# A ten-block transformer kernel: products with ones and with the rotary permutation as two rounded passes

## What is computed

```python
for i in range(2):                       # first block
    x = layer_norm(ALPHA*x + 0.5*swiglu(x, ...))
    x = layer_norm(ALPHA*x + token_mix(x, ...))
    x = layer_norm(ALPHA*x + 0.5*swiglu(x, ...))
    x = layer_norm(ALPHA*x + sigmoid(x @ w_gate + b) * (p[i] @ w_proj))
for l in range(2):                       # second block
    h = x @ w_in[l]                      # MLA and differential attention
    ...
    x = layer_norm(ALPHA*x + merged @ w_out[l])
```

```python
def l2_normalize(t):
    return t * rsqrt(sum(t*t, axis=-1, keepdims=True) + 1e-6)
```

```python
rot = concat([x1*cos - x2*sin, x2*cos + x1*sin])
```

## Time and profile before

| | us |
|---|---|
| median of 3 launches | 1514.75 (1513.74 to 1515.01) |
| the profiled execution, its own time | 1514.83 |
| its span, first to last instruction | 1513.0 |
| TensorE busy | 1496.9 |
| VectorE busy | 947.8 |
| ScalarE busy | 811.1 |
| GpSimd busy | 250.5 |

### The profile page before, as it was taken

One profiled execution on the slowest core, in us unless ns is written; L12 is line 12 of the kernel. 1 busy time (PEld: TensorE's weight loads), 2 busy tenths in 40 slices (PEclk: granted clock), 3 DMA queues, 4 the chain that ended last, 5 costly groups with the idle time before them and its releaser, 6 DMA issues.

```text
span 1513.0 us, 27372 instructions
## 1 busy us (share of the span) xinstructions
PE 1496.9 (99%) x11622; PEld 1384.2 (91%) x11622; DVE 947.8 (63%) x1379; ACT 811.1 (54%) x1249; POOL 250.5 (17%) x140
## 2 busy tenths in 40 slices
PE   9999999999999999999999999999999999999998
PEld 8998898889998889998898989998789999899997
DVE  6655466776555475654558685655477766767756
ACT  6554376545544364554574554544365675555762
POOL 0000252113000260000432040000430004500041
PEclk9999999999999999999999999999999999999999
DMA  9655464236555456555543155555455344553341
GB/s 384 226 195 194 159 210 143 79 110 229 190 196 195 167 204 222 195 195 190 195 173 113 59 190 200 194 195 195 167 209 195 112 140 152 208 188 136 131 149 56
DMA packets 39720, 266.26 MB, mean 176 GB/s; under 512 B 4460, under 2 KB 4716, under 8 KB 9392
## 3 DMA queue, kind: packets, MB, share of 16 engines
q1 hardware_dynamic: 38304, 260.13, 48.8%
q0 software_dynamic: 720, 3.35, 0.6%
q10 hardware_dynamic: 576, 1.05, 0.2%
HBM read 263.46 MB, written 1.05 MB: 175 GB/s over the span
## 4 chain that ended last, share of the span: by engine, by line
PE 94%; DVE 4%; ACT 1%; DMA 0%; issue 0%; SPq 0%; DVEq 0%
PE PS L487 17%; PE PS L488 17%; PE PS L489 16%; PE PS L501 6%; PE PS L503 6%; PE PS L502 6%; PE PS L559 4%; PE PS L562 4%; PE PS L560 4%; PE PS L470 1%; PE PS L471 1%; PE PS L472 1%; PE PS L614 1%; PE PS L1942 1%; DVE rawL L319 1%; PE PS L1351 1%
## 5 line engine op out<-in xcount | busy, mean ns | idle before, releaser
L487 PE MATMUL PS<-xTH,WH 128*128 128x256 f32 x2256 | 641.2, 284 | 0.0
L488 PE MATMUL PS<-xTL,WH 128*128 128x256 f32 x2256 | 628.7, 279 | 0.0
L489 PE MATMUL PS<-xTH,rawL 128*128 128x256 f32 x2256 | 626.6, 278 | 0.0
L316 ACT ACTIVATE WH<-raw 128x1024 fp32r<-128x1024 f32 (+2 forms) x476 | 484.6, 1048 | 131.1 <-PE PS L562 101.3
L319 DVE TENSOR_TENSOR rawL<-raw,WH 128x1024 fp32r<-128x1024 f32 (+1 forms) x395 | 481.4, 1245 | 102.5 <-ACT WH L316 102.2
L487 PEld LDWEIGHTS PS<-xTH,WH 128*128 128x128 f32 x2256 | 423.6, 188 | 9.2 <-issue 6.7
L488 PEld LDWEIGHTS PS<-xTL,WH 128*128 128x128 f32 x2256 | 423.7, 188 | 3.4 <-issue 2.9
L489 PEld LDWEIGHTS PS<-xTH,rawL 128*128 128x128 f32 x2256 | 424.9, 188 | 0.0
L319 POOL TENSOR_TENSOR rawL<-raw,WH 128x1024 fp32r<-128x1024 f32 (+1 forms) x81 | 196.1, 2443 | 1049.8 <-ACT WH L316 1049.8
L316 ACT ACTIVATE sg<-PS 128x256 f32<-128x256 f32 x79 | 30.3, 384 | 177.6 <-PE PS L489 177.6
L319 DVE TENSOR_TENSOR hh<-PS,sg 128x256 f32<-128x256 f32 x79 | 33.5, 424 | 144.7 <-ACT sg L316 144.7
(11 more groups left out here) (366 smaller groups left out, 2004.7 us busy)
## 6 DMA issues: line engine op xcount, KB each, us to landing
raw<-in_weights SPq DMA_DIRECT2D x233, 1024.0 KB, 4.8
gb<-in_lngb SPq DMA_DIRECT2D x16, 512.0 KB, 5.1
raw<-in_weights SPq DMA_DIRECT2D x2, 1056.0 KB, 4.9
gb<-in_ln SPq DMA_DIRECT2D x4, 512.0 KB, 4.5
cst<-in_consts POOLq DMA_DIRECT2D x1, 1378.5 KB, 10.4
x0T<-in_xT ACTq DMA_DIRECT2D x4, 256.0 KB, 5.5
raw<-in_weights SPq DMA_DIRECT2D x4, 256.0 KB, 5.1
xt<-in_x POOLq DMA_DIRECT2D x1, 1024.0 KB, 17.3
```

The source lines that it names most:

```text
L316: return Q.put("act", waits, lambda e: e.activation(out, in_, func, **kw))
L487: e.matmul(out, c, xTH[:, k, :], start=k == 0, stop=False)
L488: e.matmul(out, c, xTL[:, k, :], start=False, stop=False)
L489: ins = e.matmul(out, u.L(i, 128 * k, 128), xTH[:, k, :], start=False, stop=k == KD - 1)
```

## The change

Both kinds of product are now made in two rounded passes. For the squares, ScalarE writes a rounded square `sqH` beside the plain one, VectorE subtracts it from the plain one in place (`sqL`), and TensorE multiplies both with the rounded ones and accumulates. For the rotation, the ScalarE copy `rw` is now the rounded part, VectorE makes the remainder `rl` from PSUM, the cosine product reads PSUM, the bank is released by the copy, the remainder and the cosine product together, and the sine product goes into a tile of its own (`rsum`). The permutation is rounded once a layer. The rounded ones are made once, at the first use, which is the first `squares`. The products with the ones at L1807 to L1809 stay as they are.

```diff
+    ones_ready = []
+
+    def ones_rounded():
+        if not ones_ready:
+            ones_ready.append(act(onesR[:, :], ones, ACT.Copy, [par_ready]))
+        return ones_ready[0]
...
-        o_ = act(onesR[:, :], ones, ACT.Copy, [par_ready])
-        ple_bias[l] = (bgR, o_, stt(bgR[:, :], bgH[:, :].bitcast(F32), C("minus1")[0:2, :], bg[:, :], ALU.mult, ALU.add, [a]))
+        ple_bias[l] = (bgR, ones_rounded(), stt(bgR[:, :], bgH[:, :].bitcast(F32), C("minus1")[0:2, :], bg[:, :], ALU.mult, ALU.add, [a]))
...
+        sqH = [put_at("sqHa", [128, 512], 63, F32R), put_at("sqHb", [128, 512], 65, F32R)]
+        sqL = [put_at("sqLa", [128, 512], 12, F32R), put_at("sqLb", [128, 512], 14, F32R)]
...
                                 if (nm, i) == ("q", 1):
-                                    a = act(sq3, dst, ACT.Square, [a, sq_free[m]])
+                                    y = act(sq3, dst, ACT.Square, [a, sq_free[m]])
                                 else:
-                                    a = tt(sq3, dst, dst, ALU.mult, [a, sq_free[m]], "pool")
-                                conv_ready[nm, i] = (m, a)
+                                    y = tt(sq3, dst, dst, ALU.mult, [a, sq_free[m]], "pool")
+                                h = act(sqH[m][:, :].rearrange("p (j s) -> p j s", j=2), dst, ACT.Square, [a, sq_free[m]])
+                                conv_ready[nm, i] = (m, y, h)
...
         def squares(nm, i):
-            m, a = conv_ready[nm, i]
+            m, y, h = conv_ready[nm, i]
             b, free = bank("B")
-            p = pe([a, free], lambda e: e.matmul(PS[:, b, :], ones, sq[m][:, :], start=True, stop=True))
+            lo = tt(sqL[m][:, :], sq[m][:, :], sqH[m][:, :].bitcast(F32), ALU.subtract, [y, h])
+
+            def fn(e):
+                e.matmul(PS[:, b, :], onesR[:, :], sqH[m][:, :], start=True, stop=False)
+                return e.matmul(PS[:, b, :], onesR[:, :], sqL[m][:, :], start=False, stop=True)
+            p = pe([ones_rounded(), h, lo, free], fn)
...
-        rw = [put_at("rwa", [128, 2, S], 36), put_at("rwb", [128, 2, S], 38)]
+        rw = [put_at("rwa", [128, 2, S], 36, F32R), put_at("rwb", [128, 2, S], 38, F32R)]
+        rl = [put_at("rla", [128, 2, S], 70, F32R), put_at("rlb", [128, 2, S], 72, F32R)]
+        rs_, permR = put_at("rsum", [128, 2, S], 74), put_at("permR", [128, 128], 76, F32R)
...
+        perm_ready = act(permR[:, :], C("perm"), ACT.Copy, [xw])
...
         def rotary(b, p, dst):
...
-            w = rw[i]
+            w, wl = rw[i], rl[i]
             a = act(w[:, :, :], v2(b), ACT.Copy, [p, rw_free[i]])
-            release(b, a)
-            c = tt(pr[:, :, :], w[:, :, :], two(C("dcos")), ALU.mult, [a, pr_free[0]])
+            lo = tt(wl[:, :, :], v2(b), w[:, :, :].bitcast(F32), ALU.subtract, [a])
+            c = tt(pr[:, :, :], v2(b), two(C("dcos")), ALU.mult, [p, pr_free[0]])
+            release(b, a, lo, c)
 
             def later():
                 b2, free = bank("B")
-                p2 = pe([a, free], lambda e: e.matmul(PS[:, b2, :], C("perm"), w[:, :, :].rearrange("p j s -> p (j s)"), start=True, stop=True))
-                s = tt(w[:, :, :], v2(b2), two(C("dsin")), ALU.mult, [p2, c])
+
+                def fn(e):
+                    e.matmul(PS[:, b2, :], permR[:, :], w[:, :, :].rearrange("p j s -> p (j s)"), start=True, stop=False)
+                    return e.matmul(PS[:, b2, :], permR[:, :], wl[:, :, :].rearrange("p j s -> p (j s)"), start=False, stop=True)
+                p2 = pe([perm_ready, a, lo, free], fn)
+                s = tt(rs_[:, :, :], v2(b2), two(C("dsin")), ALU.mult, [p2, c])
                 release(b2, s)
-                y = tt(dst, pr[:, :, :], w[:, :, :], ALU.add, [s, c])
+                y = tt(dst, pr[:, :, :], rs_[:, :, :], ALU.add, [s, c])
```

## The result

The changed kernel takes 1545.31 us (median of 4 launches, 1544.61 to 1546.13), the kernel before 1514.88 in the same comparison: a ratio of 1.0203, 95% interval 1.0185 to 1.0220. It is 30 us slower. The forecast was 1539.6 us with a range of 1532 to 1548.

The account below looks back on a forecast made before the run. TensorE, busy 1496.9 of 1513.0 us, was taken as the bound. Mixer waits less savings gave +24.6 us, the second block +0.2; on the profiled 1514.83 us that made 1539.6 us, range 1532 to 1548.

Parts of the forecast that it names:

- The savings per product: Squares and rotary products: two passes take 0.46 us in place of 0.86, saving 0.40 each, 6.4 us for all 16.
- The rival with 0.42 us a pass: All changed products: passes no cheaper, at 0.42 us each, giving 1545.7 us; chance 0.05.
- The four waits: TensorE before the four squares products of each mixer layer: 2.4, 4.3, 4.3 and 3.15 us, waiting for VectorE's remainder.
- The sum of 24.8 us: Whole kernel: 24.6 us added by two mixer layers plus 0.2 us by the second block.
- The remainder's price of 0.69: VectorE's subtraction in the mixer: 0.69 us, as a multiplication of the same size with both inputs in SBUF.
- the dearer one of 1.21: Mixer remainders at 1.21 us, as where a GpSimd product ran: 4.2 us on top for all eight, 1543.8 us.
- The second block: Rotary products: waits of 1.7 us against savings of 1.6 a layer, +0.2 us over both layers.
- The bank wait: Before the second value product: 1.3 us a layer, its PSUM bank being kept until remainder and cosine product are through.
- TensorE's busy time: Whole kernel: about 6 us less TensorE busy time while the span grows by 25.
- The clock: Rival: TensorE's clock falls in the mixer stands, at most 3.0 us a fall, 1543 to 1552 us; chance 0.27.
- the forecast's own signs: Wrong if waits before squares are under 2 us, not spent on the convolution group, or the clock falls below 1.00 mid-kernel.
- The faster case: Rival: VectorE's remainders ready before TensorE comes, so all 16 savings stand and nothing else, 1508.4 us; chance 0.04.

Follow-up runs that it names:

- e4: e1 without the VectorE subtraction, the second pass multiplying the rounded square again (sums not those of the squares): 1514.35 us, ratio 1.0003.
- e9: e5 with GpSimd's weight remainders in this stretch given back to VectorE: 1516.61 us, ratio 1.0020.
- e12: Control: the kernel before, with GpSimd's weight remainders in this stretch given to VectorE: 1516.48 us, ratio 1.0018.
- e1: The mixer part of the change alone (squares products), rotation as in the kernel before: 1544.69 us, ratio 1.0205.
- e2: The rotation part of the change alone (rotary products), squares as in the kernel before: 1515.14 us, ratio 1.0008.
- e3: The changed kernel with useless TensorE products put in front of each squares product, in the time it would stand: 1539.65 us, ratio 1.0171.
- e5: e1 with each VectorE subtraction issued right behind its two squares, ahead of the convolution steps: 1529.62 us, ratio 1.0097.

## Why the forecast held, and the step that failed

**The direction and the mechanism** were right: the remainder's place behind six convolution steps makes TensorE stand. e4 shows it by taking away the subtraction, e9 beside its control e12 by changing its place, and e1 and e2 that the rotation adds next to nothing.

**The savings per product.** 0.86 to 0.46 us was right in both parts (1182.37 to 1182.61 is a pass of 0.24 in the trace of the changed kernel, 223.52 to 223.83 in e3 is 0.31: the first pass after a wait costs 0.08 more). The rival with 0.42 us a pass is out.

**The four waits.** 2.4, 4.3, 4.3 and 3.15 us were forecast; e3, at full clock, has 2.4, 4.3, 4.3 and 2.9. The sum of 24.8 us has its measurement in e3's ratio 1.0171, 25.8 us. The remainder's price of 0.69 was right (0.68); the dearer one of 1.21 did not occur in the changed kernel, and in e5 it turned out to be no bound at all.

**The second block.** +0.2 us was forecast, e2 gives +1.2 with an interval that holds 0. The bank wait was drawn at 1.3 and is 0.95 on average, in e2.

**TensorE's busy time** was to fall by about 6 us and rose by 8.0. The low clock is in that: without its 13 us of slow running (7.1 in the first mixer layer, 5.9 in the second) it would be 5 us less, and in e2 and e4 it is 2.3 and 5.0 us less.

**The clock is the step that failed.** The forecast kept the clock up and gave its fall a chance of 0.27, because the row at the end of the kernel shows it falling after some 5 us of idling. That row gives one instance and was read as a threshold. Here stands of 4.15 us brought it down in all four cases, one of 2.28 us too, and one of 2.27 not; in e5 it fell after stands of 1.86, 1.79 and 2.11. The price named for that case, 1543 to 1552, holds the measured 1545.3. By two of the forecast's own signs it was wrong: the clock fell in the middle of the kernel, and the wait in front of the fourth product was under 2 us. The low clock hid that fourth wait: TensorE at half speed arrived when the operand was ready, so the 6 us of both fourth waits are inside the 13 us of slow running. That the two offset each other, and the time stayed inside the range, was luck: the forecast drew the waits and the clock as sums that add. The Trainium skill, "TensorE: Matmul & The Clock Gate", section "HAM oscillation — how this bites in real kernels", warns of just this exchange, waits that make the work after them run at half clock; the trace agrees, with a granted clock of 0.50 from 244.2 to 251, of which TensorE worked from 245.2 on.

**The faster case** was priced wrongly: not 1508.4, since e4 shows that the mixer's share of the savings becomes a wait behind ScalarE's chain. The row that said so was among the rows: 0.26 us idle before L1303, a wait already reached in the kernel before. In the forecast sum its disappearance was rightly booked as a gain, because TensorE came so late; in the faster case, with the savings and no waits, it grows to 1.8 us.

What stays open: what decides whether a short stand brings the clock down. The first stand of 2.3 us did so in the first layer of the changed kernel and not in the second; in e1, with the same mixer code, it did so in the second (2.27 us) and not in the first (2.27). Length alone does not decide it. Open too is whether the mixer's savings could be had with a shorter norm chain on ScalarE, which was not tried.

## What to carry to other kernels

A cheaper product is worth its saving only if its operand is ready as early as before; when a change adds an operand that another engine makes, look in that engine's list for what stands ahead of it, and above all for work that itself waits for the product's own engine. A stand of TensorE costs more than its length, because the work behind it may run at half clock. And before booking a saving, look for the next wait that is already touching the path: a few tenths of idle time there can swallow everything that is saved in front of it, as the 3.2 us in e4.

## What the runs showed of the hardware

VectorE and GpSimd did not share: a VectorE instruction with both inputs in SBUF that began 0.07 us behind a GpSimd one of 2.4 us stood until that was over (2.85 us in place of 0.68, 3.42 in place of 1.22), and without GpSimd's instructions the effect is gone (e9). In the other order GpSimd pays: its square took 1.84 us in the changed kernel, beside VectorE's weight remainder begun 0.28 us earlier, and 1.04 in e5 where VectorE stood idle:

```profile
223.53 1.84 POOL L319 TENSOR_TENSOR sqb<-kq 128x512 f32<-128x512 f32 x1 [1.22 <-ACT kq L316]
```

```profile
226.39 1.04 POOL L319 TENSOR_TENSOR sqb<-kq 128x512 f32<-128x512 f32 x1 [3.69 <-ACT kq L316]
```

The Trainium skill, "SBUF — State Buffer", section "Who interferes with whom", states both: who begins first has the shared ports for the whole instruction, and the other one waits; the trace agrees, with 2.85 us in place of 0.68 where GpSimd was first and 1.84 in place of 1.04 where VectorE was. By these rows a start moved by a tenth of a microsecond could cost two; no run moved one by so little.

TensorE's clock, once down, stayed down for 3.4 to 6 us of work without a gap in the changed kernel, and whether a stand of 2.3 us brings it down differed between two layers with the same program, and between the changed kernel and e1.
